# First attention of a two-block transformer kernel: heads projected in pairs, rotated columns of four heads in one product, shared-key scores in fp32r

## What is computed

```python
# 8 "own-key" heads: each head has its own 64 key columns, 32 rotated columns are shared by all keys
q = (rmsnorm(c_q, g_q_lat) @ w_uq).reshape(B, T, 8, 64 + 32)      # c_q: T x 384
q_nope, q_pe = q[..., :64], q[..., 64:]
q_pe = apply_rope(q_pe, cos_b, sin_b)
kv = (rmsnorm(c_kv, g_kv_lat) @ w_ukv).reshape(B, T, 8, 64 + 64)  # c_kv: T x 256
k_nope, v = kv[..., :64], kv[..., 64:]
k_pe = apply_rope(k_rope, cos_b, sin_b)                            # one for all heads
s = (q_nope . k_nope + q_pe . k_pe) * 96 ** -0.5, causal, softmax, times v

# 8 "shared-key" heads (all use the same 64-wide key and value), only the 128 keys
# with the largest index score per query are kept
att = einsum(q, k_selected) * 64 ** -0.5, softmax, times v_selected
```

## Time and profile before

| What | Value |
|---|---|
| median of three runs | 2655.59 us (2651.74 to 2656.82) |
| time of the profiled execution | 2656.64 us |
| its span, first to last instruction | 2654.8 us |
| mean granted clock | 0.991 |
| busy: PE, DVE, ACT, POOL | 98%, 51%, 28%, 14% |
| first attention: start of the first projection | 560.1 us |
| first attention: end of the last product with V | 729.3 us |

### The profile page before, as it was taken

How to read it: one execution, slowest core, us unless ns; L and a number is a source line. 1 busy time by engine, 2 the same in 40 slices (tenths; PEclk the granted TensorE clock), 3 DMA queues, 4 the chain that set the end, 5 groups by cost and what they waited for, 6 DMA issues and landing times.

```text
span 2654.8 us, 33223 instructions
## 1 busy us (share of the span) xinstructions
PE 2601.8 (98%) x12356; PEld 2100.3 (79%) x12356; DVE 1347.7 (51%) x1959; ACT 754.3 (28%) x1032; POOL 368.5 (14%) x306
## 2 busy tenths in 40 slices
PE   8999999988999999999999999999999999999998
PEld 6888887655488888888888888888887768888887
DVE  7666655577657643364434434444226663433334
ACT  4222232355532321331111111322322452322223
POOL 1111123000021010131001001103001104110112
PEclk9999999989999999999999999999999999999999
DMA  6454433110035333333333332233331013233331
GB/s 190 145 143 142 139 107 94 38 37 17 1 118 151 111 97 93 102 89 95 96 94 95 95 95 67 61 110 89 86 111 41 13 50 96 81 95 95 95 91 67
DMA packets 358032, 241.21 MB, mean 91 GB/s; under 512 B 14768, under 2 KB 356144, under 8 KB 357936
## 3 DMA queue, kind: packets, MB, share of 16 engines
q1 hardware_dynamic: 357936, 239.92, 30.7%
HBM read 237.79 MB, written 2.10 MB: 90 GB/s over the span
## 4 chain that ended last, share of the span: by engine, by line
PE 93%; DVE 3%; ACT 2%; issue 1%; POOL 0%; DMA 0%; DVEq 0%; SPq 0%; ACTq 0%; POOLq 0%
PE PS L816 23%; PE PS L823 23%; PE PS L818 23%; PE PS L793 4%; PE PS L796 4%; PE PS L794 4%; PE PS L1284 2%; PE PS L1075 1%; PE PS L1276 1%; PE PS L1114 1%; PE PS L1121 1%; PE PS L984 1%; PE PS L748 1%; DVE VA L1691 1%; PE PS L1085 0%
## 5 line engine op out<-in xcount | busy, mean ns | idle before, releaser
L816 PE MATMUL PS<-NH,WH 128*128 128x512 f32 (+1 forms) x2112 | 615.4, 373 | 3.6 <-DVE WL L1670 1.8
L818 PE MATMUL PS<-NH,WL 128*128 128x512 f32 (+1 forms) x2112 | 613.5, 372 | 0.0
L823 PE MATMUL PS<-NL,WH 128*128 128x512 f32 (+1 forms) x2112 | 585.4, 372 | 0.0
L1670 DVE TENSOR_TENSOR WL<-RAW,WH 128x2048 fp32r<-128x2048 f32 x189 | 471.9, 2497 | 109.7 <-ACT WH L1315 109.3
L1315 ACT ACTIVATE WH<-RAW 128x2048 fp32r<-128x2048 f32 x189 | 361.7, 1914 | 498.9 <-PE PS L823 491.7
L823 PEld LDWEIGHTS PS<-NL,WH 128*128 128x128 f32 x2112 | 385.4, 189 | 71.3 <-POOL NL L2303 0.7
L818 PEld LDWEIGHTS PS<-NH,WL 128*128 128x128 f32 x2112 | 385.3, 188 | 70.8
L816 PEld LDWEIGHTS PS<-NH,WH 128*128 128x128 f32 x2112 | 382.8, 188 | 73.6 <-issue 5.4
L2261 POOL CAST HH<-VA 128x512 f32 (+2 forms) x88 | 60.4, 686 | 1305.0 <-DVE VA L1831 1305.0
L1389 ACT ACTIVATE SA<-PS 128x512 f32<-128x512 f32 x104 | 62.1, 597 | 628.9 <-PE PS L823 595.7
L816 PE MATMUL PS<-HH,WH 128*128 128x512 f32 (+1 forms) x820 | 238.1, 371 | 0.0
(11 more groups left out here) (345 smaller groups left out, 2631.2 us busy)
## 6 DMA issues: line engine op xcount, KB each, us to landing
RAW<-in_ffn_w_in SPq DMA_DIRECT2D x88, 512.0 KB, 5.0
MW<-in_w_mod SPq DMA_DIRECT2D x72, 512.0 KB, 3.5
RAW<-in_w_in SPq DMA_DIRECT2D x70, 512.0 KB, 4.3
RAW<-in_w_gate SPq DMA_DIRECT2D x44, 512.0 KB, 4.0
RAW<-in_w_up SPq DMA_DIRECT2D x44, 512.0 KB, 5.3
RAW<-in_w_down SPq DMA_DIRECT2D x32, 512.0 KB, 4.2
RAW<-in_ffn_w_out SPq DMA_DIRECT2D x32, 512.0 KB, 4.2
RAW<-in_w_out SPq DMA_DIRECT2D x16, 512.0 KB, 4.0
```

The source lines that it names most:

```text
L816: pe.matmul(outs[half][x], w[half][0], xh(k), start=i == 0, stop=False)
L818: pe.matmul(outs[half][x], w[half][1], xh(k), start=False, stop=False)
L823: last = pe.matmul(outs[half][x], w[half][0], xl(k), start=False, stop=i == kn - 1)
L1670: dve.tensor_tensor(WL[1 - s][:, :], RAW[1 - s][:, :], WH[1 - s][:, :].bitcast(F32), ALU.subtract).then_inc(w_lo, 1)
```

## The change

1. **Rotated columns together.** The weight block is loaded so that the 32 rotated query columns of four heads lie side by side. `rope_product` makes one 128-row product (9 matmuls), ACT copies it once, PE permutes it once, DVE multiplies by cosine and sine and adds once. SP then carries each head's 32 rows to its place in `QB` with a DMA (`rotated`, 64 KB each).
2. **Own-key heads in pairs.** `key_product` (6 matmuls) and `query_product` (9) each make two heads at once, 64 rows each. So even heads use rows 0 to 63 for the plain columns and 64 to 95 for the rotated; odd heads use 64 to 127 and 32 to 63, with rows 0 to 31 zero, and contract over 128 rows. ACT copies the queries, DVE the keys, in halves of 64 rows.
3. **Order.** The first four heads' products stand before unit 0. Those of the second four are spread: on PE after the scores of units 12, 13, 14 and 15; on ACT and DVE at the ends of the iterations named in the diff. The split of the next weight block is a step of its own (`split_next`): the first before unit 0, the second at the end of iteration u = 14.
4. **Shared-key scores in fp32r.** POOL splits `QA` and `KA` into high and low, while the own-key units run. SP moves 64-row halves in three DMA steps each for two pairs of heads, so that one operand holds high in one half of the rows and low in the other. A score is then two fp32r matmuls: one over 128 rows, one over 64 rows with the low part of the key.
5. The rotated rows of `KB` come by four DMAs instead of POOL copies; ACT loads the table of the exponential before its first copy.

Below are the new functions and their places, in the order SP, PE, ACT, DVE, POOL. What they replace, `project` on three engines and the one call for `w_out` on SP, is in the functions printed above.

```diff
+                for k in range(3):
+                    rows = w_uq[k * P:(k + 1) * P, n * 384:(n + 1) * 384].rearrange("p (h c) -> p h c", h=4)
+                    for c0, c1, at in ((64, 96, 256), (0, 64, 0)):
+                        sp.dma_start(RAW[s][:, k * 384 + at:k * 384 + at + 4 * (c1 - c0)]
+                                     .rearrange("p (h c) -> p h c", h=4), rows[:, :, c0:c1]).then_inc(w_loaded[s], 16)
...
+            sp.wait_ge(norm_lo, norm_kv.lo + 2)
+            for i in range(4):
+                sp.dma_start(KB[rope_rows(i), i, :], KPE[64:96, :]).then_inc(pe_key, 16)
+            def rotated(n, i):
+                sp.dma_start(QB[rope_rows(i), i, :], SF[32 * i:32 * i + 32, T:2 * T]).then_inc(pe_query[i], 16)
+            pairs(wo_b, 1, inp["w_out"][0], 0, KD, 0, True)
+            sp.wait_ge(pj_rot, 1)
+            for i in range(4):
+                rotated(0, i)
+            for j in range(0, 4, 2):
+                for i in (j, j + 1):
+                    sp.wait_ge(qa_lo, i + 1)
+                    sp.dma_start(qa_spare(i).bitcast(F32), two_halves(QAR[0:64, i, :]).bitcast(F32)).then_inc(qa_out, 16)
+                sp.wait_ge(qa_out, 16 * (j + 2))
+                for i in (j, j + 1):
+                    sp.dma_start(two_halves(QAR[0:64, i, :]).bitcast(F32), qa_high(i)[64:128].bitcast(F32)).then_inc(qa_in, 16)
+                sp.wait_ge(qa_in, 16 * (j + 2))
+                for i in (j, j + 1):
+                    sp.dma_start(qa_high(i)[64:128].bitcast(F32), qa_spare(i).bitcast(F32)).then_inc(qa_back, 16)
+                sp.wait_ge(qa_back, 16 * (j + 2))
+            pairs(wo_b + 1, 1, inp["w_out"][0], 0, KD, 2 * P, True)
+            sp.wait_ge(pj_rot, 2)
+            for i in range(4):
+                if i == 3:
+                    sp.wait_ge(at_s, 16)
+                rotated(1, i)
+            pairs(wo_b + 2, KD // 2 - 2, inp["w_out"][0], 0, KD, 4 * P, True)
...
+            def rope_product(n):
+                s = (pj_b + n) % 2
+                begin(pj_b + n)
+                if n:
+                    pe.wait_ge(pj_query_out, 4 * n)
+                for k in range(3):
+                    c = k * 384 + 256
+                    wh, wl = (z[s][:, c:c + P] for z in (WH, WL))
+                    last = three(B[6][:, :], wh, wl, NH[:, k, 0:T], NL[:, k, 0:T], k == 0, k == 2)
+                last.then_inc(pj_rope, 1)
+            def key_product(n, p):
+                s = (pj_b + n) % 2
+                if n or p:
+                    pe.wait_ge(pj_key_out, 4 * n + 2 * p)
+                for k in range(2):
+                    c = 1152 + k * 256 + p * P
+                    last = three(B[7][:, :], WH[s][:, c:c + P], WL[s][:, c:c + P],
+                                 NH[:, (3, 7)[k], 0:T], NL[:, (3, 7)[k], 0:T], k == 0, k == 1)
+                last.then_inc(pj_key, 1)
+            def query_product(n, p):
+                s = (pj_b + n) % 2
+                if p:
+                    pe.wait_ge(pj_cos, n + 1)
+                elif n:
+                    pe.wait_ge(pj_query_out, 4 * n - 2)
+                for k in range(3):
+                    c = k * 384 + p * P
+                    wh, wl = (z[s][:, c:c + P] for z in (WH, WL))
+                    last = three(B[5 + p][:, :], wh, wl, NH[:, k, 0:T], NL[:, k, 0:T], k == 0, k == 2)
+                last.then_inc(pj_query, 1)
+            def rope_swap(n):
+                pe.wait_ge(pj_y, n + 1)
+                if n:
+                    pe.wait_ge(pj_rot, n)
+                    pe.wait_ge(at_o, 1)
+                else:
+                    pe.wait_ge(px16, 2)
+                pe.matmul(B[4][:, :], PX16, SF[:, 0:T], start=True, stop=True).then_inc(pj_sw, 1)
+            def projected(n):
+                pe.wait_ge(pj_query, 2 * n + 2)
...
+            def own_key(u):
+                h = UNITS[u][1]
+                if u == 0:
+                    pe.wait_ge(pe_key, 16 * 4)
+                    pe.wait_ge(b_zero, 2)
+                pe.wait_ge(pj_key_out, h + 1)
+                pe.wait_ge(pj_query_out, h + 1)
+                pe.wait_ge(pe_query[h % 4], 16 * (h // 4 + 1))
             def scores(u):
                 if u >= 2:
                     pe.wait_ge(at_m, u - 1)
                 q, k, keys = q_scores(u)
-                pe.matmul(B[u % 2][:, 0:keys], q, k, start=True, stop=True).then_inc(at_s, 1)
+                if UNITS[u][0] == "b":
+                    if u % NT == 0:
+                        own_key(u)
+                    pe.matmul(B[u % 2][:, 0:keys], q, k, start=True, stop=True).then_inc(at_s, 1)
+                    return
+                if u == 32:
+                    pe.wait_ge(ka_done, 1)
+                    pe.wait_ge(qa_back, 16 * 4)
+                pe.matmul(B[u % 2][:, 0:keys], q, k, start=True, stop=False)
+                pe.matmul(B[u % 2][:, 0:keys], q[0:64], KAL[0:64, 0:keys], start=False, stop=True).then_inc(at_s, 1)
...
+            rope_product(0)
+            key_product(0, 0)
+            query_product(0, 0)
+            rope_swap(0)
+            key_product(0, 1)
+            query_product(0, 1)
             for u in range(-AHEAD, len(UNITS)):
-                if u + AHEAD in (0, 16):
-                    project((u + AHEAD) // 16)
                 if u + AHEAD < len(UNITS):
                     scores(u + AHEAD)
+                if u + AHEAD == 0:
+                    projected(0)
+                elif u + AHEAD == 12:
+                    rope_product(1)
+                    key_product(1, 0)
+                elif u + AHEAD == 13:
+                    query_product(1, 0)
+                elif u + AHEAD == 14:
+                    rope_swap(1)
+                    key_product(1, 1)
+                elif u + AHEAD == 15:
+                    query_product(1, 1)
+                elif u + AHEAD == 16:
+                    projected(1)
...
+            def rope_copied(n):
+                act.wait_ge(pj_rope, n + 1)
+                if n == 0:
+                    act.wait_ge(ix_acc, len(INDEX))
+                else:
+                    act.wait_ge(pj_sw, n)
+                act.activation(SF[:, 0:T], B[6][:, :], ACT.Copy).then_inc(pj_y, 1)
+            def queries_copied(n, p):
+                act.wait_ge(pj_query, 2 * n + p + 1)
+                for i in (2 * p, 2 * p + 1):
+                    if n:
+                        act.wait_ge(at_s, 4 * i + 4)
+                    act.activation(QB[half_rows(i), i, :], B[5 + p][half_rows(i), :], ACT.Copy).then_inc(pj_query_out, 1)
...
+            act.activation(warm[:, :], eps[:, :], ACT.Exp)
+            rope_copied(0)
+            split_next(0)
+            queries_copied(0, 0)
+            queries_copied(0, 1)
...
+                if u + AHEAD == 12:
+                    rope_copied(1)
+                elif u + AHEAD == 14:
+                    queries_copied(1, 0)
+                elif u + AHEAD == 16:
+                    queries_copied(1, 1)
+                elif u + AHEAD == 17:
+                    split_next(1)
...
+            def rope_cos(n):
+                dve.wait_ge(pj_y, n + 1)
+                own.settle(dve, dve.tensor_tensor(RB[:, :], B[6][:, :], TB[:, 0, :], ALU.mult))
+                dve.sem_inc(pj_cos, 1)
+            def rope_sum(n):
+                dve.wait_ge(pj_sw, n + 1)
+                if n:
+                    for i in range(4):
+                        dve.wait_ge(pe_query[i], 16 * n)
+                own.settle(dve, dve.tensor_tensor(SF[:, T:2 * T], B[4][:, :], TB[:, 1, :], ALU.mult))
+                dve.tensor_tensor(SF[:, T:2 * T], SF[:, T:2 * T], RB[:, :], ALU.add).then_inc(pj_rot, 1)
+            def keys_copied(n, p):
+                dve.wait_ge(pj_key, 2 * n + p + 1)
+                for i in (2 * p, 2 * p + 1):
+                    if n:
+                        dve.wait_ge(at_s, 4 * i + 4)
+                    dve.tensor_copy(KB[half_rows(i), i, :], B[7][half_rows(i), :]).then_inc(pj_key_out, 1)
...
+            rope_cos(0)
+            keys_copied(0, 0)
+            split_next(0)
+            rope_sum(0)
+            keys_copied(0, 1)
...
+                if u + AHEAD == 13:
+                    rope_cos(1)
+                    keys_copied(1, 0)
+                elif u + AHEAD == 14:
+                    rope_sum(1)
+                elif u + AHEAD == 15:
+                    keys_copied(1, 1)
+                elif u + AHEAD == 17:
+                    split_next(1)
...
+            pool.wait_ge(at_s, 4)
+            for j in range(4):
+                pool.tensor_copy(qa_high(j), two_halves(QA[:, j, :])).then_inc(qa_hi, 1)
+                pool.wait_ge(qa_hi, j + 1)
+                pool.tensor_tensor(two_halves(QAR[:, j, :]), two_halves(QA[:, j, :]), qa_high(j).bitcast(F32),
+                                   ALU.subtract).then_inc(qa_lo, 1)
```

(48 more changed lines are left out.)

103 lines of the change are left out of this document (34 added, 69 removed).

## The result

The changed kernel takes 2636.16 us in the median of four runs (2634.50 to 2638.22), the kernel before 2655.11. The ratio is 0.9929, with a 95% interval of 0.9917 to 0.9941: 18.95 us faster. Forecast were 2634 and a gain of 21.7. The profiled execution takes 2638.22 us (span 2636.4), 18.42 less than the one of before.

What follows compares the result with a forecast made beforehand. PE, 93% of the span, was taken to bound the kernel, with ACT and DVE pacing some units. Gains 9.8 + 6.4 + 5.5 = 21.7 us gave 2635 profiled, 2634 in the median; range 2625 to 2644 (8 in 10).

Steps and rivals of the forecast that it cites:

- Part A: First projection: less PE work, first mask at 572.6 instead of 582.37; gain 9.8 us (7.4 to 10.2).
- Part B: Second projection, first to second product with V: 27.8 us instead of 34.17, gain 6.4.
- 4.1 us of new stop: Before the second product with V: PE waits for the chain behind iteration 14's weight split on ACT and DVE.
- The projection's own 8.8: Second projection: PE work of 9.84 us less its own filled stop of 1.07, net +8.8.
- Rival 2: Iteration 14's split is hidden, ACT and DVE being ahead of PE: 2634 - 4.1 = 2630 us; chance 15%.
- The lower bound of this part: Second projection: gain of about 2.7 us if no PE stop is filled and the new stop has its full 5.3 + 1.0.
- Part C: Shared-key scores as two fp32r matmuls: 11.1 us less on PE, of which 5.5 count (2.5 to about 9).
- Costed at nothing: POOL's splits (13 us), SP's six waiting steps (some 13 us), weight-block DMAs and 128-row contraction: no cost in time.
- rival 4: SP's queue: second four's rotated rows wait behind six shared-key steps; 10 us slower, 2665.6, at 7.0 a landing; chance 5%.
- Rival 1: Granted clock falls for 15 us as PE stands still; product with V +4.6, units +2.9: 2641.5 us; chance 15%.
- A granted clock under 1 after 565: In the profile after: one of three named signs that the prediction is wrong.
- the stretches that it called unchanged at 14.9: Own-key units from one product with V to the next, without a projection: 14.9 us each, as before.

Runs made afterwards that it cites:

- e1: The changed kernel with the output projection's weight split moved on ACT and DVE from iteration 14 to 16; 2633.8 us, ratio 0.9917.
- e3: The changed kernel with shared-key scores back to one fp32 call, without POOL's splits and SP's moves of halves; 2644.0 us, ratio 0.9958.
- e5: e1 with the first projection's sine steps ahead of DVE's split and the second pair's keys behind the second mask; 2630.4 us, ratio 0.9912.
- f1: e5 with the keys' copy back ahead of the first mask and the exponential's table loaded behind ACT's first query copies; 2629.7 us, ratio 0.9896.
- e4: The changed kernel with the second projection in one piece before unit 16's scores, the split inside it; 2630.9 us, ratio 0.9910.
- e8: e7 with one useless PE product in each of the iterations -3 to 7; 2630.2 us, ratio 0.9912.
- f2: f1 with one useless PE product in each of the iterations -3 to 7 and 13 to 15; 2628.4 us, ratio 0.9897.
- e7: e4 with sine steps ahead of DVE's split and second-pair keys behind the second mask in both projections; 2631.5 us, ratio 0.9914.

## Why the prediction was right, and where it was off

**Part A**, 9.8 forecast, 9.23 measured. Its chain is the one above: DVE's sine steps end at 570.77 (forecast 570.0; 0.4 of the difference is the later start, most of the rest the two key copies, 0.7 each instead of 0.6). The landing took 1.96 instead of 1.9, and the ramp from the first mask to the first product with V 12.76 instead of 12.61, where the forecast had no change. The Trainium skill's "DMA: Bandwidth & Descriptors" (the anatomy of one DMA), for DMAs that POOL issues, gave an estimate of 2.15; the 1.96 of SP's DMA lies between the forecast's 1.9 and that.

**Part B**, 27.8 forecast, 27.50 measured. Both of its terms hold. The 4.1 us of new stop are shown by e1: the split gone, 3.86 gone (of the whole stop of 4.11 it leaves 0.26). The projection's own 8.8 is what e1 leaves over a plain stretch, 23.64 - 14.94 = 8.70. Rival 2, the hidden split, is out. The lower bound of this part was added up wrongly, without effect: 34.17 - 14.94 - 9.84 - 6.3 is 3.1 and not 2.7.

**Part C**, 5.5 forecast, 5.93 measured and 5.95 by e3: 1.97 up to the product at unit 48 (forecast 1.4 + 0.7, where 1.34 and 0.2 had been added to 1.4 instead of 1.5) and 3.96 from there (3.4). A score of 512 keys costs more than forecast: its second matmul starts 0.41 behind the first, the transposes 0.43 behind that, so 0.84 instead of 0.56, where the fp32 call took 1.05. The transposes, 0.47 up to the next score before, now take 0.30. Together a unit with three of them takes PE 1.14 instead of 1.53: 0.39 saved and not 0.49. It did no harm, since DVE set the pace, as part C said. The timeline of PE:

```profile
684.84 0.48 PE L1180 MATMUL PS<-KAR,NH 128*128 128x512 f32 x1
685.25 0.49 PE L1181 MATMUL PS<-KAL,NH 64*128 64x512 f32 x1
685.68 0.55 PE L1191 MATMUL PS<-ident,VA 128*128 128x128 f32 x3
685.98 0.48 PE L1180 MATMUL PS<-KAR,QAR 128*128 128x512 f32 x1
```

The same in the kernel before:

```profile
700.63 1.12 PE L1075 MATMUL PS<-KA,QA 64*128 64x512 f32 x2
701.69 0.55 PE L1085 MATMUL PS<-ident,VA 128*128 128x128 f32 x3
702.16 1.12 PE L1075 MATMUL PS<-KA,QA 64*128 64x512 f32 x2
```

**Costed at nothing.** SP's six steps took 19.4 us (577.57 to 596.96, where SP goes on) instead of 13: a landing is 2.3 to 2.4 for 128 KB and issuing two takes 1.2. The second four's rows were issued at 601.1, when they were ready, so rival 4 was never near.

**The term that was wrong** is the clock, held at full in the forecast. Rival 1 named the mechanism and the place, at 15%, and 7.5 us; it came, at 3.0, since the clock was down for 6.8 us and not for 15, and 0.7 of them lay over the stop. A granted clock under 1 after 565 was also what the prediction named as a sign of being wrong, and of the stretches that it called unchanged at 14.9 one took 17.97. The total came near because this price was small and not because the clock stayed up; how much of the fall lies over the product is chance, 1.57 to 3.04 us in the four profiles. 21.7 - 3.0 (clock) - 0.6 (part A) + 0.3 (B) + 0.4 (C) - 0.4 (later start) = 18.4, the difference of the profiled executions. The rule of the Trainium skill's "TensorE: Matmul & The Clock Gate" ("Why this matters for your kernels"), that idle gaps bring the half clock back, should have had the larger chance: the four profiles with the long stop unfilled agree. e1 adds that it can happen after stops of 0.39 and 1.30 only, and e5 and f1 that it doesn't always.

**Not tried, so open.** What holds the clock at half from 532 on ahead of the attention in both kernels, and what ends it sooner or later. It is where the 0.39 us come from: at 510 the profile after was 1.9 us ahead (the one of before had a granted clock of 0.71 and 0.86 at 384 to 392, this one 1.00), and it lost them here, where the one of before has 1.00 from 548 on the earlier trace rows. Windows of the changed kernel:

```profile
544.00:548.00 4.00, 2.56 (x6) 1.82 (x6) 3.54 (x6) 1.55 (x3) 1.83 (x2) 0.50 0.16 40
548.00:552.00 4.00, 4.00 (x13) 2.57 (x12) 1.04 (x2) 1.46 (x4) 0.00 (x0) 0.56 0.10 25
```

## What to carry to other kernels

A large step on a side engine (here a weight split of 1.9 and 2.3 us) is put where PE has a long product of its own to do, not where a tiny step behind it, here a reciprocal of 0.16, feeds that product. Price a stop of PE twice: its length, and the slower work after it. And before a block of work is spread over a pipeline, time it in one piece: here the plain form cost little more than PE's own work (10.07 and 9.84), was 5.5 us better than the spread one with the split misplaced, and 0.85 worse than the spread one with the split moved.

## What the runs showed of the hardware

In thirteen profiles of the changed kernel and its variants the granted clock fell at a few places, but not in each: between the first score and the first product with V in six, around or soon after the second product in seven. A fall cost 0.4 to 3.0 us there. Over the second product it cost half of the part of it that lay over PE's work, and nothing for the part that lay over a stop. Two profiles of the same kernel so differ by 1.5 in a stage whose instructions and waits are alike. That the falls are also why one kernel's runs scatter, by 1.1 us in e4 and by 10.0 in e1, is likely and not shown: of the other runs only the mean clock is known (in e1 0.986 in the slowest and 0.990 in the fastest, but 0.988 in all four of `after`, which differ by 3.7). Seven useless products in a stop went with a full clock in the one profile that has them. What single ones strewn over the iterations do is open, since in e8 and f2 they did not stand where e7 and f2 had their falls.
